# A two-block transformer on one core: convolution taps reordered with first taps on ScalarE, norm sums before the retention, and a local attention with split copies and mask products

## What is computed

```python
u = a * sigmoid(b)
y = conv(u, conv_w, 31 taps, causal, per channel) + conv_b
y_conv = silu((y - mean(y)) * rsqrt(var(y) + EPS) * ln_w + ln_b)
y = retention(rq, rk, rv, positions)          # rotary, decayed scores, a state carried along
y_ret = silu(rg) * groupnorm(y) * ret_gn_w
h = h + concat(y_conv, y_ret) @ w_out
```

```python
s_loc = where(abs(i - j) <= WINDOW, q @ k_loc.T * scale, -inf)
p = softmax(concat(sink, q @ k_ctx.T * scale, s_loc))
out = p_ctx @ v_ctx + p_loc @ v_loc
```

## Time and profile before

| what | value |
|---|---|
| median of 3 executions | 2569.56 us (2565.83 to 2570.19) |
| the profiled execution: its own time / its span | 2569.9 us / 2568.3 us |
| PE, DVE, ACT, POOL busy, of the span | 95%, 64%, 41%, 8% |
| mean granted TensorE clock | 0.981 |
| waits of PE in the first 360 us, longest group | 11.5 us, for DVE's low part of the retention |
| last tap of the convolution ends | 265.55 us |
| first product of w_out | 340.44 us |
| local attention, first score product to first w_out product | 1672.97 to 1831.65 us |

### The profile page before, as it was taken

The page is one execution under the profiler, slowest core; times in us unless marked ns, Lnnn a source line. Parts: engine busy times, 40 slices in busy tenths (PEclk is TensorE's granted clock), DMA queues, the critical chain, the costliest instruction groups (busy, mean ns, idle before and its releaser), DMA issues.

```text
span 2568.3 us, 30658 instructions
## 1 busy us (share of the span) xinstructions
PE 2434.6 (95%) x12001; PEld 1992.2 (78%) x12001; DVE 1632.4 (64%) x2049; ACT 1061.3 (41%) x1537; POOL 214.4 (8%) x226
## 2 busy tenths in 40 slices
PE   7999789999999999999999999988995999999996
PEld 6787578888888877888787898855684888888885
DVE  6999746225243645454443871477556999999987
ACT  4224334334131121121212522177343777777765
POOL 1000420000000000101000100000103111111100
PEclk9999899999999999999999999999996999999998
DMA  4111022220111223232322321100227899999988
GB/s 150 65 43 37 21 107 74 76 98 24 41 50 62 86 84 106 78 119 82 100 88 70 124 78 33 50 34 17 84 90 270 332 387 387 393 395 394 398 333 307
DMA packets 116348, 370.38 MB, mean 144 GB/s; under 512 B 6309, under 2 KB 15701, under 8 KB 116240
## 3 DMA queue, kind: packets, MB, share of 16 engines
q1 hardware_dynamic: 94832, 293.63, 30.0%
q0 software_dynamic: 21408, 75.24, 9.3%
HBM read 343.63 MB, written 25.26 MB: 144 GB/s over the span
## 4 chain that ended last, share of the span: by engine, by line
PE 82%; DVE 12%; ACT 3%; issue 2%; DMA 1%; SPq 0%; POOLq 0%; ACTq 0%; DVEq 0%
PE banks L431 24%; PE banks L433 24%; PE banks L432 24%; DVE conv_out L1525 4%; DVE w_lo L425 2%; PE banks L536 1%; PE banks L2520 1%; PE banks L2387 1%; PE banks L2366 1%; ACT w_hi L418 1%; DVE w_max L1913 1%; PE banks L2569 1%; DMA expert_w<-in_w_up 1%; PE banks L2665 1%; PE banks L2646 0%
## 5 line engine op out<-in xcount | busy, mean ns | idle before, releaser
L2047 DVE TENSOR_TENSOR expert_w_lo<-expert_w,expert_w_hi 128x2048 fp32r<-128x2048 f32 x189 | 427.0, 2287 | 30.3 <-ACT expert_w_hi L1365 29.0
L1365 ACT ACTIVATE expert_w_hi<-expert_w 128x2048 fp32r<-128x2048 f32 x192 | 367.1, 1918 | 150.9 <-PE banks L433 130.2
L431 PE MATMUL banks<-act_hi,w_hi 128*128 128x512 f32 x960 | 376.5, 392 | 7.3 <-DVE w_lo L425 4.2
L432 PE MATMUL banks<-act_lo,w_hi 128*128 128x512 f32 x960 | 374.5, 390 | 0.0
L433 PE MATMUL banks<-act_hi,w_lo 128*128 128x512 f32 x960 | 374.5, 390 | 0.0
L418 ACT ACTIVATE w_hi<-w_raw 128x1024 fp32r<-128x1024 f32 x152 | 157.1, 1058 | 297.5 <-PE banks L433 297.4
L425 DVE TENSOR_TENSOR w_lo<-w_raw,w_hi 128x1024 fp32r<-128x1024 f32 x152 | 182.3, 1225 | 140.5 <-ACT w_hi L418 136.1
L431 PE MATMUL banks<-w_hi,act_hi 128*128 128x512 f32 (+1 forms) x640 | 245.8, 384 | 6.6 <-DVE w_lo L425 2.9
L433 PE MATMUL banks<-w_hi,act_lo 128*128 128x512 f32 (+1 forms) x640 | 243.3, 380 | 0.0
L432 PE MATMUL banks<-w_lo,act_hi 128*128 128x512 f32 (+1 forms) x640 | 242.8, 379 | 0.0
L431 PEld LDWEIGHTS banks<-act_hi,w_hi 128*128 128x128 f32 x960 | 180.8, 188 | 47.8 <-issue 4.2
(11 more groups left out here) (408 smaller groups left out, 4076.6 us busy)
## 6 DMA issues: line engine op xcount, KB each, us to landing
expert_w<-in_w_gate SPq DMA_DIRECT2D x32, 2048.0 KB, 11.5
expert_w<-in_w_up SPq DMA_DIRECT2D x32, 2048.0 KB, 12.1
expert_w<-in_w_down SPq DMA_DIRECT2D x32, 2048.0 KB, 12.2
ada_w<-in_w_ada POOLq DMA_DIRECT2D x48, 512.0 KB, 4.1
w_raw<-in_mlp_up_w SPq DMA_DIRECT2D x16, 1024.0 KB, 5.3
w_raw<-in_mlp_down_w SPq DMA_DIRECT2D x16, 1024.0 KB, 5.0
w_raw<-in_w_in SPq DMA_DIRECT2D x10, 1024.0 KB, 5.4
w_raw<-in_w_in SPq DMA_DIRECT2D x18, 512.0 KB, 6.2
```

The lines of the kernel that those rows point to most:

```text
L431: nc.tensor.matmul(o_, lh, rh, start=start, stop=False)
L432: nc.tensor.matmul(o_, lh, rl, start=False, stop=False)
L1365: act.activation(EWH[ring][:, 2 * j:2 * j + 2, :], EW[slot][:, 2 * j:2 * j + 2, :], ACT.Copy).then_inc(w_hi, 1)
L2047: dve.tensor_tensor(EWL[slot][:, c, :], EW[slot][:, c, :], EWH[ring][:, c, :], ALU.subtract).then_inc(w_ready, 1)
```

## The change

**Convolution.** The first tap of each half (weight and bias) goes to ACT, right after the gated half; DVE has 138 tap instructions left. The angles move up between the first two gated halves, half taps are taken channel by channel for the second half of the tokens, and the counts of taps between other steps change.

```diff
-CONV_OPS = 4 * TAPS + 2 * HALF_TAPS
+CONV_OPS = 4 * (TAPS - 1) + 2 * (HALF_TAPS - 1)
 (ACT)
+            def first_tap(i):
+                c, part, h = CONV_ORDER[i]
+                if part == "a":
+                    act.wait_ge(acc_dve, freed(T_C + i)[1])
+                    act.activation(YC[:, c, h * 512:(h + 1) * 512], U[:, c, h * 512:(h + 1) * 512], ACT.Identity,
+                                   scale=VT[:, c, 0:1], bias=VT[:, c, 31:32]).then_inc(conv_1, 1)
             for i in range(7):
                 sigmoid_half(i)
+                first_tap(i)
             split_hi(1)
             for i in range(7, 14):
                 sigmoid_half(i)
+                first_tap(i)
+                if i == 11:
+                    act.wait_ge(trig, 1)
+                    act.activation(CS1[:, :, :, :], ANK[:, :, :, :], ACT.Sin).then_inc(trig, 1)
+            sigmoid_half(14)
             split_hi(2)
+            first_tap(15)
             split_hi(3)
 (DVE)
             gated_half(1)
+            angles()
             gated_half(3)
-            half_taps(HALF_TAPS, (0, 1), 0)
+            half_taps(HALF_TAPS - 1, (0, 1), 0)
             gated_half(5)
-            angles()
+            half_taps(HALF_TAPS - 1, (0,), 1)
             split_lo(1)
             gated_half(7)
-            half_taps(HALF_TAPS, (0, 1), 1)
+            half_taps(HALF_TAPS - 1, (1,), 1)
+            conv_taps(3, [0, 1])
...
             dve.wait_ge(trig, 2)
+            conv_taps(5, [0, 1, 2])
             for t in range(NT):
...
-                    conv_taps(2, [0, 1, 2, 3])
-            conv_taps(28, [0, 1, 2, 3])
+                    conv_taps(3 - t % 2, [0, 1, 2, 3])
+            conv_taps(31, [0, 1, 2, 3])
             split_lo(4)
-            conv_taps(CONV_OPS - taps_n[0] - 4, [0, 1, 2, 3])
+            conv_taps(CONV_OPS - taps_n[0], [0, 1, 2, 3])
```

```diff
+        MEANB = BK[5], BK[7]
 (PE)
+            ln_mean_sum(0)
             ret_scores(0)
             ret_T(1)
+            ln_mean_sum(1)
             for t in range(NT):
...
                 if t in (0, 1):
-                    ln_mean_sum(t)
-                if t in (2, 3):
-                    ln_var_sum(t - 2)
+                    ln_var_sum(t)
 (DVE)
+            ln_center(0)
             ret_mask(0)
+            ln_center(1)
             for t in range(NT):
...
-                if t in (0, 1):
-                    ln_center(t)
+                if t in (1, 2):
+                    ln_recip(t - 1)
                 if t in (3, 4):
-                    ln_recip(t - 3)
-                if 1 <= t < 5:
-                    split_lo(B_WO, js=(t - 1,))
-                if t in (6, 7):
-                    ln_low(t - 6)
+                    split_lo(B_WO, js=(2 * t - 6, 2 * t - 5))
+                if t in (5, 6):
+                    ln_low(t - 5)
 (ACT)
             ret_copy(1)
+            ln_square(0)
+            ln_square(1)
             for t in range(NT):
                 if t + 2 < NT:
                     ret_copy(t + 2)
+                if t in (1, 2):
+                    ln_sqrt(t - 1)
...
-                if t in (5, 6):
-                    ln_out(t - 5)
+                if t in (4, 5):
+                    ln_out(t - 4)
 (POOL)
-                if t in (3, 4):
-                    ln_scale(t - 3)
+                if t in (2, 3):
+                    ln_scale(t - 2)
```

```diff
+    P3 = at("w_probs_third", [P, 640], F32, O_R + 29 * K)
+    PB = [P2[:, 0, :], P2[:, 1, :], P3[:, :]]
 (PE)
-                if 2 <= v <= 65:
-                    y = v - 2
+                if 3 <= v <= 66:
+                    y = v - 3
                     pe.wait_ge(at_e, y + 1)
-                    if y >= 1 and y % 2 == 0:
-                        pe.wait_ge(at_c, y // 2)
-                    elif y >= 1:
-                        pe.wait_ge(at_ca, (y + 1) // 2)
-                    for n in range(5 if 0 < y // 8 < 7 else 4):
-                        m = pe.transpose(PAIR[2][:, n * P:(n + 1) * P], P2[:, y % 2, n * P:(n + 1) * P], IDN)
+                    if y >= 1:
+                        pe.wait_ge(at_ca, y)
+                    for n in range(FRONT):
+                        m = pe.transpose(probs_at(n), probs_of(y)[:, n * P:(n + 1) * P], IDN)
                     m.then_inc(at_t, 1)
+                    if y >= 1:
+                        pe.wait_ge(at_c, y)
+                    for n in range(FRONT, key_blocks(y)):
+                        m = pe.transpose(probs_at(n), probs_of(y)[:, n * P:(n + 1) * P], IDN)
+                    m.then_inc(at_tb, 1)
...
-                        seeded = v >= SEEDED and dst < 512
-                        beside = [i for i, kt in enumerate(near) if kt != t and dst < 512 and not seeded]
-                        if seeded:
-                            pe.wait_ge(at_mkd if v % 2 else at_mka, (v - SEEDED) // 2 + 1)
+                        beside = [i for i, kt in enumerate(near) if kt != t and dst < 512]
 (ACT)
+        def front_probs(y):
+            act, g = nc.scalar, y // 4
+            act.wait_ge(at_t, y + 1)
+            if g >= 2:
+                act.wait_ge(at_o, g - 1)
+            act.activation(PT4[:, g % 2, 0:FRONT, y % 4, :], PAIR[2][:, 0:FRONT * P].rearrange("p (n q) -> p n q", n=FRONT),
+                           ACT.Copy).then_inc(at_ca, 1)
 (DVE)
+        def back_probs(y):
+            dve, g, n = nc.vector, y // 4, key_blocks(y)
+            dve.wait_ge(at_tb, y + 1)
+            if g >= 2:
+                dve.wait_ge(at_o, g - 1)
+            dve.tensor_copy(PT4[:, g % 2, FRONT:n, y % 4, :],
+                            PAIR[2][:, 512:512 + (n - FRONT) * P].rearrange("p (n q) -> p n q", n=n - FRONT)).then_inc(at_c, 1)
```

More of the change, by code:

```diff
@@ L678, in build @@
         u2_pad, c2_n, c2_hi, c2_lo = sem("short_conv_pad_then_token_tiles"), sem("short_conv_ops_then_chosen"), sem("short_conv_hi"), sem("short_conv_lo")
-        at_s, at_m, at_e, at_t, at_c, at_ca, at_o = (
-            sem("wa_" + s) for s in ("scores", "max", "exp", "probs_T", "copied_dve", "copied_act", "out_T"))
+        at_s, at_m, at_e, at_t, at_tb, at_c, at_ca, at_o = (
+            sem("wa_" + s) for s in ("scores", "max", "exp", "probs_T_front", "probs_T_back", "copied_dve", "copied_act", "out_T"))
+        FRONT = 3
         at_sx, at_es, at_rl, at_rt, at_rb, at_on, at_hi, at_lo = (
@@ L1288, in _ @@
             conv_hi(1)
-            for v in range(64 + 15):
+            for v in range(64 + 16):
                 if v == 2:
@@ L1306, in _ @@
                     act.wait_ge(at_m, x + 1)
-                    if x >= 2:
-                        act.wait_ge(at_t, x - 1)
-                    act.activation(P2[:, x % 2, 0:w], scores_of(x), ACT.Exp, bias=NM2[:, x:x + 1], scale=AD ** -0.5,
+                    if x >= 3:
+                        act.wait_ge(at_tb, x - 2)
+                    act.activation(probs_of(x)[:, 0:w], scores_of(x), ACT.Exp, bias=NM2[:, x:x + 1], scale=AD ** -0.5,
                                    accum_out=L2[:, x:x + 1]).then_inc(at_e, 1)
-                    if x % 2 == 0 and SEEDED <= x + 2 < 64:
-                        if x + 2 == SEEDED:
-                            act.wait_ge(at_mk, 1)
-                        act.wait_ge(at_e, x + 1)
-                        act.activation(local_scores(x + 2), masks_of(x + 2), ACT.Copy).then_inc(at_mka, 1)
                     if h == 7:
@@ L1324, in _ @@
                     act.activation(RLT[:, :], BK[6 + (t + 1) % 2][:, :], ACT.Copy).then_inc(at_rb, 1)
-                if v >= 15 and (v - 15) % 8 == 0 and v < 64 + 15:
-                    t = (v - 15) // 8
+                if v >= 16 and (v - 16) % 8 == 0 and v < 64 + 16:
+                    t = (v - 16) // 8
                     act.wait_ge(at_on, t + 1)
@@ L1507, in gated_half @@
                                       YC[:, c, h * 512:(h + 1) * 512], ALU.mult).then_inc(acc_dve, 1)
-            taps_done = [[0, 0] for _ in range(4)]
+            taps_done = [[1, 1] for _ in range(4)]
             last_tap = [[0, 0] for _ in range(4)]
@@ L1899, in _ @@
                     conv_lo(0)
-            for v in range(64 + 16):
+            for v in range(64 + 17):
                 if v == 2:
@@ L1907, in _ @@
                     query_lo(v // 8 + 2)
-                if 2 <= v <= 65 and v % 2 == 1:
-                    probs_copy(v - 2, dve.tensor_copy, dve, at_c)
+                if 3 <= v <= 66:
+                    back_probs(v - 3)
                 if v < 64:
@@ L1934, in _ @@
                                     ).then_inc(at_rl, 1)
-                if v >= 14 and (v - 14) % 8 == 0 and v < 64 + 14:
-                    t = (v - 14) // 8
+                if v >= 15 and (v - 15) % 8 == 0 and v < 64 + 15:
+                    t = (v - 15) // 8
                     dve.wait_ge(at_rb, t + 1)
@@ L2503, in _ @@
             pe.wait_ge(kz_zero, 2)
-            for v in range(64 + 11):
-                if v % 8 in (7, 1) and 7 <= v < 50:
-                    t, kv = (v - 7) // 8, (v - 7) % 8 // 2
```

(7 more changed lines are left out.)

84 lines of the change are left out of this document (30 added, 54 removed).

## The result

| what | before | after |
|---|---|---|
| median (range) | 2569.88 us (2565.83 to 2570.28, 4 executions) | 2547.30 us (2545.93 to 2548.43, 4 executions) |
| ratio, 95% interval | | 0.9915, 0.9898 to 0.9933 |
| the profiled execution: own time / span | 2569.9 / 2568.3 us | 2545.9 / 2544.3 us |
| PE, DVE, ACT, POOL busy | 95%, 64%, 41%, 8% | 96%, 63%, 42%, 8% |
| last tap of the convolution ends | 265.55 us | 243.67 us |

The last four lines say where the 24.0 us of span went: 15.25 ahead of w_out, 1.16 just behind it (before, the transposes of tile 7 waited there once more), 7.11 in the attention, 0.48 at the end.

The account below looks back on a forecast made before the run. TensorE is busy 95% of the span, so only its standstills pay. From 2569.9 us, -15.0 (convolution and retention) and -6.2 (attention) give 2548.7; the median shown is 0.3 lower, so 2548.5, range 2539 to 2560.

Parts of the forecast that it names:

- -15.0: Convolution and retention: w_out would start at 325.4 us against 340.4; bounds -20.5 to -4.4 us.
- -6.2: Local attention: tiles, last 12 heads, start and end together would save 6.2 us; bounds -14 to +4.
- 50.9 of work, idle 8.5: Retention: from 265.5 us VectorE's queue would hold 50.9 us of work and 8.5 idle, ending at 324.9.
- no stretch at the lower clock: Retention: TensorE would go on at once after the gate, without the 7.7 us wait or slow clock.
- Rival B: Retention: ScalarE's SiLU blocks hold its queue, 5.5 us more show, w_out at 331, 2554 us; chance 0.13.
- Rivals C: Retention: idle time stays near 19 us, only the tail is hidden, w_out at 336, 2559 us; chance 0.07.
- D: Convolution: first taps queue behind gated halves and taps still end after the projection; 2564 us; chance 0.03.
- at the end the inverse sums' transposes waited 0.97 ...: -1.5: Attention's end: these transposes would stand ahead of the last head's copy, split over two engines, saving 1.5 us.
- The mask term: Attention: masks move to TensorE as products, adding 0.12 us a head, 0.96 us a tile.
- the 1.0 us of waits that go: Attention tile: waits for exp and copies, 1.0 us, go since transposes run a step later with three buffers.
- rival A: Attention: it gives nothing because masks and waits eat the gain; 2554.7 us; chance 0.15.
- Rival E: Attention: TensorE's clock stays at 1.2 of 2.4 GHz, 1.4 us a head, throughout 2638 us; chance 0.02.

Follow-up runs that it names:

- the kernel with both parts: The kernel after with the attention of before, so convolution and retention parts together; ratio to before 0.9950, attention 160.52 us.
- whole copies: The kernel after, but transposed numerators copied whole, even heads by ACT, odd by DVE; ratio to before 0.9933, tile 19.67 us.
- mask copies: The kernel after, but from head 10 on ACT or DVE copies write the mask before the scores; ratio to before 0.9931, tile 20.17 us.

## Why the prediction was right, step by step

Predicted 2548.5 us, measured 2547.3; the range held it with room on both sides. In the sum, -15.0 stood against a measured -15.25 and -6.2 against -7.11; the 1.2 us behind w_out was not counted at all. Between the two profiles the gain is 24.0 us where 21.2 were forecast, between the medians 22.6: the profiled execution of after is the fastest of its four.

**Convolution.** "The last ends at 212.9 + 26 x 1.20 = 244.1": 212.49 + 31.18 = 243.67. The counts of 31 and 26 and the dependent half taps at 0.79 (9 in 7.05, 0.78 each) came out. Two details did not. I expected ScalarE's first taps to be hidden; four waits of VectorE for them, 2.9 us in all, three of them 0.9, show that VectorE arrives right behind its own gated half each time. And w_lo of the second block came 0.4 earlier instead of later. Neither reached TensorE: it waits 3.8 us for w_lo ahead of 256, as before. The run with the first taps on VectorE shows that a last tap 2 us later costs nothing.

**Retention.** The layout was "50.9 of work, idle 8.5"; measured 50.2 and 9.1, and even its halves held (4.5 forecast in tiles 0 to 2, 4.6 measured; 4 forecast for the SiLU blocks, 4.3 measured). One phrase failed: "no stretch at the lower clock" holds for the mean sums but not for the stage, whose granted clock rose only from 0.87 to 0.88; it did not matter since VectorE's queue was the path. What made the forecast possible is that only one queue decides there, and each of its instructions had a duration in the profile of before. Rival B, that ScalarE closes the retention by 5.5 us more, is out: its two waits are those that I had counted. The Trainium skill (ScalarE: Activation LUTs, What ACT_TABLE_LOAD costs) counts some 2.7 us for a load with its drain; removing one measured 1.40. The 1.29 us that the prediction read from the earlier trace rows show only what lies behind a load's start; the removal shows both sides of it. Rivals C (idle near 19) and D (late taps) did not come.

**Attention.** The total of -6.2 was near the measured -7.1, but partly by luck. By landmarks: to the scores of head 14 I had 1.8 and 3.2 us came, and against the kernel with both parts 5.1, since the clock costs 1.8 us more there; five tiles, 1.4 expected and 2.3 measured (19.15 a tile where I had 19.35, since the query transposes' wait is 0.96 and not 1.07 and the rest of the tile's own work was a little less than 2.44); from head 54 to w_out, 3.0 expected and 1.5 measured. The step that failed is "at the end the inverse sums' transposes waited 0.97 ...: -1.5". That wait did go, but an extra step of the pipeline also has to be drained: behind the last head's scores stand the transposes of three heads, not two, and from there to w_out it takes 10.1 us as against 10.3. The mask term (+0.12 a head) was exact: 1.86 became 1.99. The reason that I gave for the 1.0 us of waits that go, the extra step and the third buffer, is not enough: with both of them in place, whole copies give 19.67 and mask copies 20.17. In the steady tile rival A, nothing gained, would have been right for each of those, and their times are near its 2554.7 too (2554.67 and 2554.12).

**Rival E**, the lower clock throughout the attention, did not come: 1.00 in every steady tile. But its mechanism works on a small scale in every profile, after the wait of 2.7 us at the start: over the first 10 us of the attention the granted clock is 0.66 in the kernel after and 0.74 before.

## What to carry to other kernels

When a stage hangs on one engine's queue, list that queue's instructions with their measured durations and count its waits one by one: here that gave 15.0 for a measured 15.25. In a software pipeline in which two engines feed a third, ask for every kind of wait which ingredient removes it, and try them together: a part of them may do nothing or harm in the steady state. Measure the filling and the draining of the pipeline apart from it: here 3.2 of the attention's 7.1 us came before head 14. And look at what stands ahead of a long-ready instruction in its queue: moving one scaling of 0.69 us to the head of its step gave 5.1 us, more than half of what the whole attention part had given.

## What the runs showed of the hardware

The granted clock fell after the same wait of 7.7 to 7.8 us in two executions of the same instructions, but stayed low for a shorter time in one, and the stage's end came 3.4 us sooner. In both it cost more than its length, and by an amount that a single profile does not fix. A table load on ScalarE cost 1.40 us where it was taken out, 1.28 of it the load. And VectorE's dependent taps of 512 columns follow each other at 0.78 us (9 in 7.05), those that change between two channels at 0.67 (17 in 11.35):

```profile
52.73 11.35 DVE L1539 SCALAR_TENSOR_TENSOR conv_out<-conv_in,vectors_T,conv_out 128x512 f32<-128x512 f32 x17 [0.23 <-ACT conv_out L1043]
```
